# First mixer: the row sums of squares taken over two rounded parts instead of fp32

## The reference, cut to what matters

```python
def _rms(x):
    return x * lax.rsqrt(jnp.mean(x * x, axis=-1, keepdims=True) + EPS)
def l2norm(x):
    return x * lax.rsqrt(jnp.sum(x * x, axis=-1, keepdims=True) + EPS)
y_r = _rms(retention_chunkwise(q_r, k_r, v_r)) * silu(g_r)
q_d, k_d = l2norm(q_d), l2norm(k_d)
y_d = rms_norm(gated_delta_chunkwise(q_d, k_d, v_d, g, beta), out_gain) * silu(g_d)
out = hn + concat([y_r, y_d]) @ w_out
```

## Time and profile before

| | us |
|---|---|
| median of 3 runs | 2651.49 |
| lowest, highest | 2650.19, 2651.52 |
| profiled execution, its own time | 2650.02 |
| its span, first to last instruction | 2648.6 |

### The profile page before, as it was taken

The page is one execution under the profiler, slowest core; times in us unless marked ns, Lnnn a source line. Parts: engine busy times, 40 slices in busy tenths (PEclk is TensorE's granted clock), DMA queues, the critical chain, the costliest instruction groups (busy, mean ns, idle before and its releaser), DMA issues.

```text
span 2648.6 us, 32191 instructions
## 1 busy us (share of the span) xinstructions
PE 2620.0 (99%) x13046; PEld 2105.5 (79%) x13054; DVE 1514.9 (57%) x2100; ACT 1143.1 (43%) x1694; POOL 160.8 (6%) x147
## 2 busy tenths in 40 slices
PE   8999999999999999999999999999999999999998
PEld 6777778888887888887777888888877778888887
DVE  4666667565778666567765554434456754534433
ACT  6444344343466433335565333322346652423322
POOL 2222010000010000000111000000001100000000
PEclk9999999999999999999999999999999999999999
DMA  4111113223322322323111322222221122222322
GB/s 171 60 61 61 61 63 105 96 96 100 110 94 96 108 96 98 101 96 104 58 63 57 102 93 95 100 96 96 96 80 56 56 80 96 96 96 98 101 96 72
DMA packets 66674, 235.38 MB, mean 89 GB/s; under 512 B 7520, under 2 KB 8160, under 8 KB 66528
## 3 DMA queue, kind: packets, MB, share of 16 engines
q1 hardware_dynamic: 63504, 228.35, 26.0%
q10 hardware_dynamic: 3024, 4.99, 0.6%
HBM read 231.21 MB, written 2.10 MB: 88 GB/s over the span
## 4 chain that ended last, share of the span: by engine, by line
PE 89%; DVE 5%; ACT 3%; issue 1%; POOL 0%; DMA 0%; SPq 0%; ACTq 0%; DVEq 0%
PE bank L472 27%; PE bank L474 27%; PE bank L473 27%; DVE w_lo_k L1502 1%; PE bank L824 1%; PE bank L845 1%; ACT w_hi_k L994 1%; PE bank L894 1%; PE bank L834 1%; DVE xr_lru L1813 0%; PE bank L912 0%; DVE kept_att L1932 0%; PE bank L902 0%; PE bank L685 0%; DVE rot_att L1960 0%
## 5 line engine op out<-in xcount | busy, mean ns | idle before, releaser
L472 PE MATMUL bank<-x_hi_k,w_hi_k 128*128 128x512 f32 x2152 | 865.7, 402 | 9.2 <-DVE x_lo_k L1509 8.3
L994 ACT ACTIVATE w_hi_k<-raw_k 128x1024 fp32r<-128x1024 f32 x431 | 454.7, 1059 | 897.2 <-PE bank L474 895.5
L474 PE MATMUL bank<-x_hi_k,w_lo_k 128*128 128x512 f32 x2152 | 840.6, 391 | 0.0
L473 PE MATMUL bank<-x_lo_k,w_hi_k 128*128 128x512 f32 x2152 | 839.6, 390 | 0.0
L1502 DVE TENSOR_TENSOR w_lo_k<-raw_k,w_hi_k 128x1024 fp32r<-128x1024 f32 x431 | 534.4, 1240 | 167.1 <-ACT w_hi_k L994 166.3
L472 PEld LDWEIGHTS bank<-x_hi_k,w_hi_k 128*128 128x128 f32 x2152 | 404.9, 188 | 106.1 <-issue 14.6
L474 PEld LDWEIGHTS bank<-x_hi_k,w_lo_k 128*128 128x128 f32 x2152 | 404.6, 188 | 86.2
L473 PEld LDWEIGHTS bank<-x_lo_k,w_hi_k 128*128 128x128 f32 x2152 | 405.2, 188 | 81.9 <-issue 4.1
L472 PE MATMUL bank<-y_hi_k,w_hi_k 128*128 128x512 f32 x1136 | 445.3, 392 | 4.2 <-DVE y_lo_k L1848 3.2
L474 PE MATMUL bank<-y_hi_k,w_lo_k 128*128 128x512 f32 x1136 | 442.2, 389 | 0.0
L473 PE MATMUL bank<-y_lo_k,w_hi_k 128*128 128x512 f32 x1136 | 442.1, 389 | 0.0
(11 more groups left out here) (319 smaller groups left out, 2277.1 us busy)
## 6 DMA issues: line engine op xcount, KB each, us to landing
raw_k<-wstream SPq DMA_DIRECT2D x431, 512.0 KB, 3.4
outT<-h_k ACTq DMA_DIRECT2D x8, 256.0 KB, 2.9
h_k<-xT SPq DMA_DIRECT2D x4, 256.0 KB, 8.1
h_k<-xT ACTq DMA_DIRECT2D x4, 256.0 KB, 7.6
decay_mix<-constants ACTq DMA_DIRECT2D x4, 256.0 KB, 2.8
vec_k<-vectors SPq DMA_DIRECT2D x1, 282.5 KB, 9.6
cos_mix<-constants SPq DMA_DIRECT2D x1, 256.0 KB, 10.0
sin_mix<-constants SPq DMA_DIRECT2D x1, 256.0 KB, 10.1
```

Source lines behind the costliest of these rows:

```text
L472: pe.matmul(dst, wh, rh, start=start, stop=False)
L473: pe.matmul(dst, wh, rl, start=False, stop=False)
L474: return pe.matmul(dst, wl, rh, start=False, stop=stop)
L994: act.activation(k.w_hi[:, u % SPLIT, :], k.raw[:, u % RAW, :], ACT.Copy).then_inc(*hi_done.mark())
```

## The change

The sixteen sums (four in each of four heads) are now taken in the projections' format. ScalarE squares as before, then copies the squares rounded to fp32r (`squares_hi`); VectorE subtracts the rounded copy from the squares (`squares_lo`, new helper `squares_low`); TensorE multiplies fp32r ones, one column `k.one` read 128 times over, with both parts into one bank (`column_sums`). The parts are put in slices of `y_hi` and `y_lo` that are free at the time. TensorE now waits for VectorE's subtraction where it waited for ScalarE's square. The column of ones is made once, by VectorE.

```diff
@@ -260,6 +260,11 @@
     k.decd, k.um, k.xs, k.inv, k.invTd = [take(n, [P, TC * HALF]) for n in ("decd", "um", "xs", "inv", "invTd")]
     k.kb, k.kt = [take(n, [P, T]) for n in ("kb", "kt")]
     k.state, k.vnew = take("state", [P, P]), take("vnew", [P, P])
+    k.one = take("one", [P, 1], F32R)
+    k.squares = {"k": k.k_sq[:], "q": k.q_sq, "ret": k.sq[:], "o": k.sq[:]}
+    at = {"k": 7, "q": 3, "ret": 7, "o": 3}
+    k.squares_hi = {n: k.y_hi[:, kk, :] for n, kk in at.items()}
+    k.squares_lo = {n: k.y_lo[:, kk, :] for n, kk in at.items()}
     k.mix_lands = [k.mpad[1][:, 3:], k.mpad[0][:, 3:], k.mpad[2][:, 3:], k.gate_d[:]]
     k.mix_lands += [k.land_r[n][:] for n in (2, 0, 1, 3)]
 
@@ -564,11 +569,15 @@
     pe.matmul(bank[6][:, 0:HEADS * TC], k.tri_le[:], g2, start=True, stop=True)
     pe.matmul(bank[7][:, 0:HEADS * TC], k.ones, g2, start=True, stop=True).then_inc(*mark("g_sums"))
 
+    def column_sums(which, hd, b):
+        one = k.one[:].to_broadcast([P, P])
+        pe.wait_ge(*dve_done.at(which + "_sq_lo", hd))
+        pe.matmul(bank[b][:], one, k.squares_hi[which], start=True, stop=False)
+        pe.matmul(bank[b][:], one, k.squares_lo[which], start=False, stop=True).then_inc(*mark(which + "_sum", hd))
+
     def norm_sums(hd, which):
 
-        src, b = (k.k_sq[:], 7) if which == "k" else (k.q_sq, 5 if hd > 0 else 3)
-        pe.wait_ge(*act_done.at(which + "_sq", hd))
-        pe.matmul(bank[b][:], k.ones, src, start=True, stop=True).then_inc(*mark(which + "_sum", hd))
+        column_sums(which, hd, 7 if which == "k" else 5 if hd > 0 else 3)
 
     first.part(8)
     pe.wait_ge(*act_done.at("tail"))
@@ -686,16 +695,14 @@
                                    start=j == 0, stop=j == TC - 1)
                 mm.then_inc(*mark("ret", hd))
             if c == 1:
-                pe.wait_ge(*act_done.at("ret_sq", hd))
-                pe.matmul(bank[3][:], k.ones, k.sq, start=True, stop=True).then_inc(*mark("ret_sum", hd))
+                column_sums("ret", hd, 3)
             if c >= 2:
                 fill.half(1)
             pe.wait_ge(*dve_done.at("vnew", hd, c))
             pe.matmul(bank[4][:, 0:P], ch(k.kt, c), k.vnew[:], start=True, stop=True).then_inc(*mark("kv", hd, c))
             pe.matmul(ch(bank[7], c), k.vnew[:], ch(k.dec, c), start=False, stop=True).then_inc(*mark("o", hd, c))
         fill.part(1 if following else 2)
-        pe.wait_ge(*act_done.at("o_sq", hd))
-        pe.matmul(bank[2][:], k.ones, k.sq, start=True, stop=True).then_inc(*mark("o_sum", hd))
+        column_sums("o", hd, 2)
         fill.rest()
 
     def mix_out_piece(n, name, at, halves=(0, 1)):
@@ -1098,6 +1105,11 @@
     act.activation(k.col["kscale"][:], k.col["gc"][:], ACT.Exp).then_inc(*mark())
     act.activation(k.col["tail"][:], k.col["tail"][:], ACT.Exp).then_inc(*mark("tail"))
 
+    def square(hd, which, src):
+        act.activation(k.squares[which], src, ACT.Square).then_inc(*mark())
+        act.wait_ge(*now())
+        act.activation(k.squares_hi[which], k.squares[which], ACT.Copy).then_inc(*mark(which + "_sq", hd))
+
     def silu(hd, which):
         j, x = {"q": (0, k.mq), "k": (1, k.mk), "v": (2, k.mv)}[which]
         x = x[hd % 2][:]
@@ -1105,7 +1117,7 @@
         act.activation(x, x, ACT.Silu).then_inc(*mark("silu", hd, which))
         if which != "v":
             act.wait_ge(*now())
-            act.activation(k.k_sq[:] if which == "k" else k.q_sq, x, ACT.Square).then_inc(*mark(which + "_sq", hd))
+            square(hd, which, x)
 
     def norm_root(hd, which):
         dst, b = (k.k_sq[:], 7) if which == "k" else (k.q_sq, 5 if hd > 0 else 3)
@@ -1163,14 +1175,14 @@
                 if following:
                     norm_root(hd + 1, "q")
                 act.wait_ge(*pe_done.at("ret", hd))
-                act.activation(k.sq, bank[2][:], ACT.Square).then_inc(*mark("ret_sq", hd))
+                square(hd, "ret", bank[2][:])
                 act.activation(k.mrot[:], bank[2][:], ACT.Copy).then_inc(*mark("ret", hd))
             if c == 1:
                 act.wait_ge(*pe_done.at("ret_sum", hd))
                 inverse_root(k.rstd[:], bank[3][:], 1.0 / DK, "ret_root", hd)
         fill.part(1 if following else 2)
         act.wait_ge(*pe_done.at("o", hd, TC - 1))
-        act.activation(k.sq, bank[7][:], ACT.Square).then_inc(*mark("o_sq", hd))
+        square(hd, "o", bank[7][:])
         act.wait_ge(*pe_done.at("o_sum", hd))
         act.wait_ge(*dve_done.at("ret", hd))
         inverse_root(k.rstd[:], bank[2][:], 1.0 / DK, "o_root", hd)
@@ -1612,6 +1624,10 @@
     def every_tile(x):
         return x.to_broadcast([P, TC, P])
 
+    def squares_low(hd, which):
+        dve.wait_ge(*act_done.at(which + "_sq", hd))
+        dve.tensor_tensor(k.squares_lo[which], k.squares[which], k.squares_hi[which].bitcast(F32), ALU.subtract).then_inc(*mark(which + "_sq_lo", hd))
+
     def norm_unit(hd, which):
         dve.wait_ge(*act_done.at(which + "_root", hd))
         if which == "k":
@@ -1621,6 +1637,9 @@
             x = k.mq[hd % 2][:]
             dve.scalar_tensor_tensor(x, x, DK ** -0.5, k.q_sq, ALU.mult, ALU.mult).then_inc(*mark("q_unit", hd))
 
+    dve.tensor_copy(k.one[:], k.ones[:, 0:1]).then_inc(*mark("one"))
+    for which in "kq":
+        squares_low(0, which)
     norm_unit(0, "k")
     norm_unit(0, "q")
     first.rest()
@@ -1696,6 +1715,8 @@
                 dve.wait_ge(*now())
                 scaled_tiles(k.expg, bank[3][:], "beta", hd, "vb", hd)
                 dve.memset(k.state[:], 0.0).then_inc(*mark("state", hd, 0))
+            if following and lev in (4, 5):
+                squares_low(hd + 1, "kq"[lev - 4])
             fill.part(share[4] + (share[3] if later else 0))
         for c in range(TC):
             dve.wait_ge(*act_done.at("us", hd))
@@ -1704,6 +1725,8 @@
             dve.wait_ge(*pe_done.at("kv", hd, c))
             dve.scalar_tensor_tensor(k.state[:], k.state[:], k.col["egl"][:, hd, c:c + 1], bank[4][:, 0:P], ALU.mult,
                                      ALU.add).then_inc(*mark("state", hd, c + 1))
+            if c == 0:
+                squares_low(hd, "ret")
             if c == 0 and following:
                 norm_unit(hd + 1, "k")
             if c == 1 and following:
@@ -1718,6 +1741,7 @@
                 fill.part()
             elif c == 3:
                 fill.part(2)
+        squares_low(hd, "o")
         fill.part(1 if following else 2)
         dve.wait_ge(*act_done.at("o_root", hd))
         dve.scalar_tensor_tensor(us[:], bank[7][:], vcol("gdn_gain"), k.rstd[:], ALU.mult, ALU.mult).then_inc(*mark())
```

## The result

The changed kernel takes 2662.43 us (median of 6, 2661.57 to 2665.29), the kernel before 2650.82 (median of 6, 2650.17 to 2651.52). The ratio is 1.0046, with a 95% interval of 1.0036 to 1.0056: 11.6 us slower, where 2662.0 and slower had been predicted. The profiled execution took 2662.91 us with a span of 2661.4.

What follows compares the result with a forecast made beforehand. TensorE, busy 2620.0 of 2648.6 us, was taken as the bound. Terms 5.8 + 2.4 - 2.4 + 0.0 + 4.9 - 0.2 = +10.5 us on the median 2651.49 gave 2662.0, range 2660 to 2664, or 2657 to 2665 with rival 1.

Steps and rivals of the forecast that it cites:

- What a sum costs: All sixteen sums: two fp32r matmuls take 0.46 us against 0.86 in fp32, saving 0.40 each; upper bound 1.72.
- rival 4: All sixteen sums: the broadcast column is slow, up to 1.72 us a sum, 20 us more, 2682; chance 0.03.
- First place: k and q sums of head 0: TensorE waits for subtractions queued behind VectorE's `w_lo` and `land_r`, +5.8 us.
- rivals 2 and 3: 2: VectorE is in time everywhere, 2645.1, chance 0.04. 3: half of the waits vanish, 2653.0 or 2656.0, chance 0.08.
- The clock behind it: After head 0's 6.4 us stop TensorE's clock falls, matmuls 0.43 us apart: +2.4 us, bounds 0 and 3.1.
- rival 1: After head 0's k and q wait: the clock stays up, total +8.1 us, 2659.6; chance 0.30.
- the stop of 0.89 us in head 3: Step on TensorE's clock: this stop in the kernel before is followed by matmuls at the normal distance of 0.23 us.
- k and q of heads 1 to 3: Six sums whose subtractions fit VectorE's idle gaps and cost nothing, each saving 0.40: -2.4 us.
- ret: Four ret sums: `vnew` queues behind subtraction and key scaling, +0.1 a head in heads 0 to 2, -0.3 in head 3: 0.0.
- o: Four o sums: subtraction behind `w_lo` delays TensorE, +1.6 us a head in heads 0 to 2 (+4.9), -0.2 in head 3.

Runs made afterwards that it cites:

- e11: Changed kernel with ret sums of heads 0 to 2 in fp32, head 0 and o remainders earlier, projection pieces ahead of those sums: 4.1 us under the kernel before.
- e1: Changed kernel with the column of ones and head 0's k and q remainders ahead of VectorE's first `w_lo`: 2657.42 us, ratio 1.0023.
- e3: Kernel before with only the k and q sums of head 0 in the new form, the other fourteen in fp32: +9.0 us.
- e6: Changed kernel without VectorE's 16 subtractions, TensorE adding the rounded part twice (remainders left out): 2646.23 us, ratio 0.9983.
- e7: Changed kernel with head 0's column and two remainders behind the first `w_lo`, ahead of `land_r` and the second: 2659.03 us, ratio 1.0034.
- e8: Changed kernel with the o remainder of heads 0 to 2 moved ahead of round 3's `land_r` and `w_lo` on VectorE: 2657.36 us, ratio 1.0026.
- e4: Kernel before with only the four o sums in the new form, the other twelve in fp32: 2656.00 us.
- e2: Kernel before with only the k and q sums of heads 1 to 3 in the new form, the other ten in fp32: -2.3 us.
- e9: Changed kernel with o sums in fp32, head 0's remainders earlier and sums later, ret remainders behind `vnew` and sums behind `kv`: 2648.4 us.

## Why the prediction was right, and where its sizes were off

**What a sum costs.** 0.46 us was right: 137.78 to 138.25 in e11 is 0.47, and each sum that was in time saved 0.37 to 0.40. The column read 128 times costs nothing extra, so rival 4 falls.

**First place.** Right in mechanism and size. Predicted +5.8 and starts held up by 6.4 us; measured 8.39 - 2.7 = 5.7 and 6.40 (printed as 6.24 idle). e1, e3, e6 and e7 each bear it out: the time follows the subtraction's place in VectorE's program, and rivals 2 and 3 fall. That the wait for ScalarE's rounded copy was not the cause is shown by e6. ScalarE has a part in the stop by another way, which the prediction had: its two copies put `w_hi` and so VectorE's `w_lo` back by 1.32 us (61.51 against 59.20, less 0.99 of start), 1.34 predicted.

**The clock behind it.** Predicted +2.4, with the choice made for the fall; measured 2.7, so rival 1 falls. The choice rested on the stop at the program's start being nearer in length than the stop of 0.89 us in head 3. That was the right side, but the two rows used told nothing of where the fall begins.

**k and q of heads 1 to 3.** -2.4 predicted, -2.33 measured, no wait: VectorE's gaps covered the subtractions.

**ret.** 0.0 predicted; 0.02, 0.01, 0.00 and -0.34 measured. The mechanism is the predicted one, `vnew` behind the subtraction and the keys' scaling; the 0.1 a head was too much by that. The changed kernel's VectorE, head 0, against the earlier trace rows:

```profile
138.26 0.69 DVE L1629 TENSOR_TENSOR y_lo_k<-sq_k,y_hi_k 128x512 fp32r<-128x512 f32 x1 [0.72 <-ACT y_hi_k L1111]
138.87 0.68 DVE L1635 TENSOR_TENSOR k_mix<-k_mix,k_sq_mix 128x512 f32<-128x512 f32 x1
139.47 0.28 DVE L1724 TENSOR_TENSOR vnew_mix<-v_mix,bank 128x128 f32<-128x128 f32 x1
```

**o.** +1.6 a head predicted, and +1.59, +1.64 and 1.6 of the 3.20 measured; head 3 -0.2 and -0.22. (The start of head 3's subtraction, 351.86, isn't what the row of `w_lo` gives, 350.66 + 1.14 = 351.80; a slip of 0.06.)

**What was missed** is a term: the clock behind the o stops. The step "the stop of 0.89 us in head 3 is followed by the normal distance" was used for one place only; three stops of 2 us, between 0.89 and 8.27, were costed at their bare length. The trace of the kernel before has a stop of nearly that length, 1.85 us at 834.80, followed by the normal distance (rows in the last section). It would have confirmed the bare length, and wrongly: one profile can't tell. In the profile one of the three was followed by the lower clock, +1.6, and the sum of the terms was +10.5 where the medians differ by 11.6. The predicted time still came out within 0.4 us, because the median of 3 runs from which it was counted, 2651.49, is 0.7 above that of all runs shown since, 2650.82. Two errors of about a microsecond stood against each other; the hit of 0.4 us is partly luck, the sign and the places are not.

## What to carry to other kernels

On an engine that runs its program in order, price an added instruction by what stands ahead of it in that program when its input becomes ready, not by its duration: sixteen subtractions made this kernel 11.6 us slower; thirteen of them, with some moved ahead of work nobody was waiting for and with matmuls put ahead of the sums, made it 4.1 us faster. Before a cheaper instruction is credited with its saving, look at what the dearer one covered (`vnew` behind the fp32 ret sum): there the saving becomes a wait. And a stop of the engine that bounds the kernel is to be costed twice, once for its length and once for the slower matmuls that may follow it.

## What was not expected of the hardware

**TensorE's clock.** All stops are of the same engine in dense surroundings. Behind 0.69 us (three times in e8), 0.89 us and 1.06 us (e1) the matmuls keep 0.23 us. Behind 1.76 us they were 0.43 apart, the lower level of 1.2 GHz, in one of three places of the changed kernel and of e4, in none of e1 and e7 (profiled executions); the cost was 1.6 us. Behind 4.51 us there were 1.7 us of it, behind 6.24 us 2.7.

The kernel before has a stop of this length itself, far behind the mixer, where no kernel changes anything. In its own profile the normal distance follows:

```profile
834.80 0.50 PE L472 MATMUL bank<-y_hi_k,w_hi_k 128*128 128x512 f32 x1 [1.85 <-DVE y_lo_k L1848]
835.14 0.40 PE L473 MATMUL bank<-y_lo_k,w_hi_k 128*128 128x512 f32 x1
...
839.21 0.50 PE L472 MATMUL bank<-y_hi_k,w_hi_k 128*128 128x512 f32 x1 [1.38 <-DVE y_lo_k L1848]
```

In e2, at the same place:

```profile
832.29 0.50 PE L478 MATMUL bank<-y_hi_k,w_hi_k 128*128 128x512 f32 x1 [1.85 <-DVE y_lo_k L1882]
...
833.44 0.63 PE L479 MATMUL bank<-y_lo_k,w_hi_k 128*128 128x512 f32 x1
833.87 0.63 PE L480 MATMUL bank<-y_hi_k,w_lo_k 128*128 128x512 f32 x1
```

Of thirteen profiles three (e2, e4, e9) have the lower clock behind this stop. Together with the mixer's, five of 25 stops of 1.76 to 1.86 us were followed by it; of the ten stops of 1.35 to 1.40 us behind this place, none. Here it cost nothing in e2 and e4 and 0.2 us in e9, for the stop of 1.38 us that comes next is missing in these three: slow matmuls ran where TensorE would have waited. So a lower mean clock of an execution doesn't tell by itself that an o stop was followed by it.

The Trainium skill, TensorE: Matmul & The Clock Gate, Part 1, says that the number of slow matmuls at a kernel's start changes from one execution to the next, because the chip's count of activity runs on its own and not with the program. The program's start agrees (slow until 13.82 us in e2, 16.74 in e4), and the two groups of times in e1 and e4, one kernel each, fit the same reading for stops. What decides in a single execution whether a stop of 1.76 us is followed by the lower level stays open, as does why e1, with the same three o stops as e4, lies in its slower group in seven of eleven executions, 3 us apart, and e4 in five, 2.4 apart.

**The printed clock** shows these stretches (0.72 and 0.83 above), while that of the program's start, where matmuls stood 0.43 apart as well, was printed as 1.00. The distance of two starts is the surer sign.
